# In a differential attention, VectorE takes the two maxima of a tile before it combines the tile two steps back

## What is computed

```python
def diff_attention(q1, q2, k1, k2, v, lam):
    scale = q1.shape[-1] ** -0.5
    def block(args):
        a1, a2 = args
        s1 = jnp.einsum('bqhd,bkhd->bhqk', a1, k1).astype(jnp.float32) * scale
        s2 = jnp.einsum('bqhd,bkhd->bhqk', a2, k2).astype(jnp.float32) * scale
        p = (jax.nn.softmax(s1, axis=-1) - lam * jax.nn.softmax(s2, axis=-1)).astype(v.dtype)
        return jnp.einsum('bhqk,bkhd->bqhd', p, v)
    return from_blocks(lax.map(block, (to_blocks(q1), to_blocks(q2))))
```

## Time and profile before

| | |
|---|---|
| median of three runs | 2196.31 us (2190.6 to 2198.88) |
| the profiled execution | 2197.94 us, its span 2196.1 us |
| TensorE busy, share of the span | 87% |
| VectorE, ScalarE, GpSimd busy | 30%, 27%, 28% |
| the differential stage | from about 268 to 328 us of the span |

### The profile page before, as it was taken

One profiled execution on the slowest core, in us unless ns is written; L12 is line 12 of the kernel. 1 busy time (PEld: TensorE's weight loads), 2 busy tenths in 40 slices (PEclk: granted clock), 3 DMA queues, 4 the chain that ended last, 5 costly groups with the idle time before them and its releaser, 6 DMA issues.

```text
span 2196.1 us, 21409 instructions
## 1 busy us (share of the span) xinstructions
PE 1912.6 (87%) x8524; PEld 1237.5 (56%) x8524; DVE 663.0 (30%) x1392; ACT 583.7 (27%) x1042; POOL 624.2 (28%) x361
## 2 busy tenths in 40 slices
PE   4999979578877887839999999988899889999997
PEld 3544337432222222318888868644587667888886
DVE  6451355411001100132899014456311212000001
ACT  3113452100000000023223134456334423222211
POOL 0002213300000000014443134455354323555542
PEclk8998999679989898969998898999999999999999
DMA  9353102569999999962233221100132112323231
GB/s 369 153 225 142 78 1 61 230 247 427 429 429 428 427 428 430 428 231 75 98 100 93 87 87 48 58 30 20 58 137 105 65 49 78 114 83 109 79 113 58
DMA packets 96387, 379.14 MB, mean 173 GB/s; under 512 B 8443, under 2 KB 37499, under 8 KB 81964
## 3 DMA queue, kind: packets, MB, share of 16 engines
q1 hardware_dynamic: 90128, 356.37, 41.7%
q0 software_dynamic: 3456, 12.58, 1.5%
q10 hardware_dynamic: 2716, 8.98, 1.0%
HBM read 357.41 MB, written 20.51 MB: 172 GB/s over the span
## 4 chain that ended last, share of the span: by engine, by line
PE 69%; DMA 17%; DVE 6%; ACT 3%; issue 2%; POOL 2%; SPq 0%; DVEq 0%; ACTq 0%; POOLq 0%
DMA slots<-in_w_expert_up 15%; PE bank L705 14%; PE bank L707 14%; PE bank L706 14%; PE bank L680 11%; PE bank L993 7%; PE bank L1191 2%; PE bank L1171 1%; PE bank L833 1%; ACT area L1691 1%; POOL low_r L2410 1%; DMA slots<-in_w_ada 1%; PE bank L751 1%; PE bank L760 1%; PE bank L1160 1%
## 5 line engine op out<-in xcount | busy, mean ns | idle before, releaser
L2410 POOL TENSOR_TENSOR low_r<-slots,high_r 128x2048 fp32r<-128x2048 f32 x87 | 400.7, 4608 | 601.1 <-ACT high_r L1375 601.1
L993 PE MATMUL bank<-slots,area 128*64 128x512 f32 x1024 | 267.3, 682 | 76.2 <-DMA slots<-in_w_expert_up 43.2
L706 PE MATMUL bank<-xl_r,high_r 128*128 128x512 f32 (+1 forms) x864 | 330.5, 383 | 0.0
L705 PE MATMUL bank<-area_r,high_r 128*128 128x512 f32 x800 | 314.2, 393 | 0.0
L707 PE MATMUL bank<-area_r,low_r 128*128 128x512 f32 x800 | 312.5, 391 | 0.0
L1375 ACT ACTIVATE high_r<-slots 128x2048 fp32r<-128x2048 f32 x87 | 166.3, 1914 | 437.3 <-PE bank L707 408.7
L993 PEld LDWEIGHTS bank<-slots,area 128*64 128x64 f32 x1024 | 80.7, 156 | 262.1 <-issue 162.1
L706 PEld LDWEIGHTS bank<-xl_r,high_r 128*128 128x128 f32 x864 | 163.3, 189 | 31.8 <-issue 0.5
L705 PEld LDWEIGHTS bank<-area_r,high_r 128*128 128x128 f32 x800 | 151.2, 189 | 31.8 <-issue 0.5
L707 PEld LDWEIGHTS bank<-area_r,low_r 128*128 128x128 f32 x800 | 150.9, 189 | 31.7
L2236 DVE SCALAR_TENSOR_TENSOR bank<-area,cols,bank 128x512 f32<-128x512 f32 x232 | 153.5, 761 | 0.0
(11 more groups left out here) (372 smaller groups left out, 2687.7 us busy)
## 6 DMA issues: line engine op xcount, KB each, us to landing
slots<-in_w_expert_gate SPq DMA_DIRECT2D x32, 2048.0 KB, 18.4
slots<-in_w_expert_up SPq DMA_DIRECT2D x32, 2048.0 KB, 19.6
slots<-in_w_expert_down SPq DMA_DIRECT2D x32, 2048.0 KB, 20.0
slots<-in_w_in SPq DMA_DIRECT2D x15, 2048.0 KB, 8.0
slots<-in_w_ada SPq DMA_DIRECT2D x11, 2048.0 KB, 12.6
slots<-in_ffn_in_w SPq DMA_DIRECT2D x22, 1024.0 KB, 6.8
slots<-in_ffn_out_w SPq DMA_DIRECT2D x5, 2048.0 KB, 7.9
slots<-in_w_out SPq DMA_DIRECT2D x4, 2048.0 KB, 8.2
```

The source lines that it names most:

```text
L705: nc.tensor.matmul(out, xh, yh, start=start and n == 0, stop=False)
L706: nc.tensor.matmul(out, xh, yl, start=False, stop=False)
L993: last = nc.tensor.matmul(banks[which][piece, :], XT[b][:, k, piece], w[side][:, k, :], start=k == 0, stop=k == KT - 1)
L2410: nc.gpsimd.tensor_tensor(low_half(m), raw_half(m), high_half(m), ALU.subtract).then_inc(s["w_low"], 1)
```

## The change

In VectorE's loop the call of combine(t - 2) moves from in front of the two maxima of tile t to behind them. Nothing else is touched, and the number of instructions is the same on every engine.

```diff
             for t in range(34):
-                if t >= 18:
-                    combine(t - 2)
                 if t < 32:
                     for n in range(first_score(t), first_score(t + 1)):
                         dve.wait_ge(s["scores_full"], n + 1)
                         nc.vector.reduce_max(nmx[:, n % 8:n % 8 + 1], banks[2 + n % 4][:, :], AX, negate=True
                                              ).then_inc(s["max_ready"], 1)
+                if t >= 18:
+                    combine(t - 2)
                 if 1 <= t < 33:
                     inverse_sums(t - 1)
```

## The result

The changed kernel takes 2217.31 us (median of 8 runs, 2213.61 to 2223.27), the kernel before 2196.32 (8 runs, 2190.6 to 2207.04). The medians lie 21 us apart. The ratio over all runs is 1.0085, its 95% interval 1.0069 to 1.01, which is slower by some 19 us, with 15 to 22 as the interval. The forecast was 2215, in a range of 2206 to 2224.

What follows compares the result with a forecast made beforehand. The prediction took a VectorE and GpSimd chain of 3.1 us a tile to bound the stage. A longer loop (10.0 us) plus clock falls (8.6) over 2197.94 gave 2216.5, forecast as 2215 us, range 2206 to 2224.

Steps and rivals of the forecast that it cites:

- What bounded the stage before: Stage of some 57 us: repeating chain of combine, two maxima, inverse sums and GpSimd's scale, 3.1 us a tile.
- What the change removes: On VectorE: the 0.82 us wait for GpSimd's scale ahead of combine, and two combinations of 1.74 us instead of 0.75.
- the two collisions: Two combinations took 1.74 us, each with GpSimd's L2417 starting at its side; removing this is worth up to 2.0 us.
- What it adds: VectorE's max(t) waits for scores(t), which stand on TensorE behind trans(t-3), which waits for combine(t-3).
- The loop over TensorE: combine(t-3), trans(t-3), scores(t), max(t), combine(t-2): 3.83 us a tile against 3.1, or 7.25 where out(h) is in the way.
- The size at full clock: Thirteen turns from combine(16) to combine(29), ten of 3.83 us and three of 7.25, shift trans(29) by 10.0 us.
- The clock: TensorE falls to 1.2 GHz in two of four groups until the next out(h), 4.3 us each, 8.6 in all.
- the row at 307.12: TensorE's trans(25): a burst after a wait of 1.38 us at full clock, read as showing that gap length matters.
- the upper bound: The clock's term with all ten short turns and the four bursts at the low clock: 22 us.
- The rival of a held clock: Same loop, but 2.4 GHz held throughout: 2206 to 2208 us, chance 0.12.
- The gain of 8 us: Rival: maxima find their scores ready and VectorE's own 2.3 us a tile bound the stage; 2188 us, chance 0.03.
- The total: 10.0 us at full clock plus 8.6 for the clock, 18.6 over the profiled 2197.94, is 2216.5; forecast 2215 us.

Runs made afterwards that it cites:

- Experiment 3: Kernel before, with the inverse sums of tile t-1 moved ahead of the maxima of tile t: 2187.91 us, ratio 0.9949.
- Experiment 7: Kernel before, with GpSimd's two subtractions (L2417) moved behind its loop: one execution, 49.6 us from trans(15) to trans(29), 4.3 less.
- experiment 2: Half the change against the kernel before: combination of tile t-2 between the two maxima of tile t; 2202.0 us, ratio 1.0008.
- experiment 4: Changed kernel, with TensorE taking scores of tile t+3 (not t+2) ahead of tile t's transposes from tile 16 on: 2185.17 us, ratio 0.994.
- experiment 5: Kernel before, VectorE's order untouched, with TensorE's scores taken one tile further ahead: 2192.15 us, ratio 0.9961.
- experiment 1: Changed kernel, with an extra unused fp32 matmul in TensorE's gap ahead of each tile's transposes from tile 18 on: 2210.78 us, ratio 1.0063.
- experiment 8: Changed kernel with scores one tile further ahead, and the product by the values behind the next tile's scores from tile 16: 2191.52 us, ratio 0.9961.

## Why the prediction was right

**What bounded the stage before.** Right: the chain of VectorE and GpSimd, 3.1 us a tile. Experiment 3 took GpSimd out and won 11.9 us in the stage, 9.6 without the old profile's fall.

**What the change removes.** Both parts came: no wait for GpSimd in the loop, and no combination of 1.74 us. Experiment 7 confirms 2.0 us for the two collisions.

**What it adds.** The loop over TensorE was the step on which all hangs, and three runs show it from three sides. With one maximum in it, it is 0.6 us shorter (experiment 2); with the scores ahead of the transposes it opens, and in the stage the change turns from a loss into a gain (experiments 4 and 5); with the clock held it stays at 3.75 (experiment 1).

**The size at full clock.** I had 3.83 us a short turn and 10.0 in all; measured are 3.75 and 9.0. The term that was too large is the combination: I took its 0.75 us from a row in which it had waited. Behind maxima it starts before they end and adds 0.67 to the chain. Over 13 turns that is the missing 1.0 us.

**The clock.** I had 8.6 us, from two falls of 4.3 each. The three profiles give 6.7, 9.5 and 7.5 above 62.9, with two stretches of low clock each. A short turn at the low level cost 1.41 more (I took 1.3), the way from trans to the maximum behind a long product 2.0 and 2.9 more (293.36 to 300.55 and 315.40 to 323.51, against 5.18; I took 2.3). The number of falls and their length was a guess from one fall, and it was lucky that all three profiles came near it. The reason given for it does not hold: the prediction read from the row at 307.12 that it depends on the length of the gap, but gaps of 2.03 us came with the lower clock and without it, and falls came behind gaps of 0.75, 1.58 and 1.41 us too (experiments 5 and 8).

The page "TensorE: Matmul & The Clock Gate" of the Trainium skill, section "HAM oscillation — how this bites in real kernels", describes bursts of matmuls between waits of some 3 to 5 us for transfers, each of which starts cold. The gaps here are shorter than its waits, so the upper bound that the prediction took from it goes further than the page. In these traces some turns were slow and others with the same gap were not, and it never held for the whole stage: each long product within it took 5.2 to 6.2 us where a fall ran into it, and the scores behind it 1.13 again.

**The rival of a held clock** would have given 2206 to 2208; experiment 1 is that case, and its median of 2210.78 lies 3 us above. **The gain of 8 us** by VectorE's own 2.3 us a tile needed TensorE's order to be another one: made so, the profile shows 2.26.

**The total.** I had 18.6 us, all of it in the stage. The stage explains 15.7, 18.5 and 16.5 us in the three profiles, 16.9 in the mean, while the ratio gives 19 and the medians differ by 21. The rest of 2 to 4 us is inside the interval (15 to 22) and inside what single executions differ by elsewhere in the program. Whether some of it belongs to the change was not settled. So the nearness of 2215 to 2217.31 is in part luck: the stage came out some 2 us below its sum, and the rest of the program, for which the sum has no term, made up for it.

## What to carry to other kernels

Before an instruction is moved past a wait, follow who produces what that wait is for: here the producer stood, on its own engine, behind a consumer of the very instruction that was moved, so a wait that had cost nothing closed a loop. Moving small independent work forward (the inverse sums, ahead of the maxima) let GpSimd's scaling run beside the maxima without closing that loop, 11 us faster than before. Two versions at 0.994 of the time before changed both sides, the consumer's order and the producer running one tile further ahead; they can't be told from that simpler one (0.9949).

## What was not expected of the hardware

TensorE in gaps of 2.03 us with bursts of 1.7 was at 2.4 GHz for whole groups of tiles and at 1.2 GHz in others, in the same kernel at the same step (short turns of 3.75 and 5.16 us). The gap just before doesn't decide it: the fall in experiment 5 came during the scores at 271.46, behind gaps of 0.70 and 0.75 us, those in experiment 8 behind gaps of 1.58 and 1.41, while two gaps of 2.12 us at the start of the stage in experiment 1 brought none. What does decide is open. A matmul whose result nobody reads, in the gap, went with a stage without falls in the one profile of the changed kernel that has it, where the three without it have two falls each. It took nothing from the loop: the way fell from 69.6 to 62.9 us.

A combination beside GpSimd's subtraction seems to be held until near the subtraction's end, rather than to run slower by a fixed share. In the earlier trace rows it started 0.07 us behind the subtraction and took 1.74 us; in experiment 2 (subtractions at 271.67 and 290.63, combinations at 272.21 and 291.37) it started 0.54 and 0.74 us behind and took 1.27 and 1.07. All three ended 0.55 us behind the subtraction's end. So of its 0.75 us some 0.2 were done beside the subtraction, whether the two overlapped for 1.19 us or for 0.52.
